# Sparse attention with items that hold both key-value heads

## The reference, cut to what matters

```python
s = jnp.einsum('bqhgd,bchd->bqhgc', q_nope, kc) * scale
_, l, e = masked_softmax(s, avail[None, :, None, None, :])
p_cmp = e / jnp.maximum(l, TINY)
o_cmp = jnp.einsum('bqhgc,bchd->bqhgd', p_cmp, vc)
...
nsa = gates[:, :, 0] * o_cmp + gates[:, :, 1] * o_slc + gates[:, :, 2] * o_win
```

## Time and profile before

| | us |
|---|---|
| median of 3 runs | 2389.52 |
| lowest, highest | 2380.57, 2398.0 |
| the profiled execution, its own time | 2398.31 |
| its span | 2396.5 |

### The profile page before, as it was taken

How to read it: one execution, slowest core, us unless ns; L and a number is a source line. 1 busy time by engine, 2 the same in 40 slices (tenths; PEclk the granted TensorE clock), 3 DMA queues, 4 the chain that set the end, 5 groups by cost and what they waited for, 6 DMA issues and landing times.

```text
span 2396.5 us, 19995 instructions
## 1 busy us (share of the span) xinstructions
PE 1824.3 (76%) x6099; PEld 884.4 (37%) x6099; DVE 1466.1 (61%) x3339; ACT 560.5 (23%) x1754; POOL 721.5 (30%) x612
## 2 busy tenths in 40 slices
PE   7998798776887779678797786779765778656675
PEld 5575455642333222133342233334321445422221
DVE  1554520386877783677469745854974555556966
ACT  1001320112232231242222311422221222222222
POOL 0031000004454542234344522433432222223452
PEclk9975556898999999889899888889987777778988
DMA  6231003409999999999999998999999988889997
GB/s 213 90 99 46 1 0 106 141 1 375 421 418 421 422 400 421 380 370 403 412 421 409 400 420 323 383 366 399 406 375 373 342 326 300 342 347 376 391 391 301
DMA packets 152163, 750.89 MB, mean 313 GB/s; under 512 B 22092, under 2 KB 54744, under 8 KB 72056
## 3 DMA queue, kind: packets, MB, share of 16 engines
q0 software_dynamic: 84480, 608.21, 62.8%
q1 hardware_dynamic: 67576, 141.41, 16.3%
HBM read 743.96 MB, written 5.60 MB: 313 GB/s over the span
## 4 chain that ended last, share of the span: by engine, by line
DMA 26%; PE 22%; DVE 17%; issue 6%; ACT 2%; SPq 1%; PEldq 1%; POOL 1%; DVEq 1%; PEld 0%; ACTq 0%; POOLq 0%
DMA uv<-in_experts_dram,slots 18%; PE ps L2261 12%; DVE uv L2169 6%; PE ps L583 3%; PE ps L1106 2%; DMA sample_cache<-in_odd_w_in_dram 2%; PE ps L1078 2%; DMA last_w<-in_odd_w_in_dram 1%; DMA sample_w<-in_peer_w_q_dram 1%; DVE acc L2183 1%; SPq L1876 1%; PEldq L2297 1%; ACT diag L2237 1%; POOL uv L2151 1%; DMA last_rows<-in_peer_sub_keys_dram 1%
## 5 line engine op out<-in xcount | busy, mean ns | idle before, releaser
L2261 PE MATMUL ps<-uv,diag 128*128 128x512 f32 (+1 forms) x1880 | 982.5, 664 | 275.7 <-ACT diag L2237 211.5
L2151 POOL DMA_INDIRECT uv<-in_experts_dram,slots x576 | 689.3, 1197 | 1487.6 <-PE ps L2261 1021.0
L2169 DVE CUSTOM_DVE_ANT_0 uv<-uv,x 128x1024 f32<-128x1024 f32 x512 | 622.5, 1225 | 295.8 <-DMA uv<-in_experts_dram,slots 236.7
L2261 PEld LDWEIGHTS ps<-uv,diag 128*128 128x128 f32 (+1 forms) x1880 | 352.8, 200 | 821.1 <-issue 473.0
L2215 ACT ACTIVATE gelu<-dot 128x2 f32<-128x2 f32 x288 | 58.6, 203 | 1098.3 <-DVE dot L2169 1098.1
L2237 ACT ACTIVATE diag<-const,wgt 128x128 f32<-128x128 f32 (+1 forms) x470 | 165.0, 387 | 9.4
L2224 ACT ACTIVATE wgt<-gate,gelu 128x1 f32<-128x1 f32 x576 | 138.0, 287 | 38.9 <-SPq L2367 14.7
L2183 DVE SCALAR_TENSOR_TENSOR acc<-uv,wgt,acc 128x1024 f32<-128x1024 f32 x101 | 129.5, 1282 | 1.0 <-ACT wgt L2224 1.0
L2169 DVE CUSTOM_DVE_ANT_0 uv<-uv,xs 128x1024 f32<-128x1024 f32 x64 | 78.1, 1225 | 76.7 <-DMA uv<-in_experts_dram,slots 75.2
L583 PE MATMUL ps<-last_w,xT 128*128 128x512 f32 x160 | 77.2, 627 | 9.2 <-DMA last_w<-in_odd_w_in_dram 7.5
L583 PE MATMUL ps<-first_w,xT 128*128 128x512 f32 x160 | 75.6, 611 | 3.1 <-DMA first_w<-in_odd_w_in_dram 3.1
(11 more groups left out here) (425 smaller groups left out, 1910.0 us busy)
## 6 DMA issues: line engine op xcount, KB each, us to landing
sample_cache<-in_cache_dil_kv_dram SPq DMA_DIRECT2D x64, 256.0 KB, 10.4
cache<-in_even_w_in_dram SPq DMA_DIRECT2D x12, 1024.0 KB, 6.8
first_w<-in_odd_w_in_dram SPq DMA_DIRECT2D x12, 1024.0 KB, 11.1
last_w<-in_odd_w_in_dram SPq DMA_DIRECT2D x12, 1024.0 KB, 12.2
sample_cache<-in_odd_w_in_dram SPq DMA_DIRECT2D x12, 1024.0 KB, 17.2
uv<-in_experts_dram,slots POOLq DMA_INDIRECT x576, 11.1
uv<-in_peer_w_q_dram SPq DMA_DIRECT2D x8, 1024.0 KB, 12.0
first_w<-in_peer_w_q_dram SPq DMA_DIRECT2D x8, 1024.0 KB, 10.2
```

The source lines that it names most:

```text
L2151: self.k.nc.gpsimd.indirect_dma_start(out=self.uv[:, s % RING, :], out_offset=None, in_=self.table, in_offset=bass.IndirectOffsetOnAxis(ap ...
L2169: ins = nc.vector.tensor_tensor_reduce(self.uv[:, s % RING, 0:D], self.uv[:, s % RING, 0:D], x, 1.0, 0.0, ALU.mult, ALU.add, self.dot[:, g ...
L2261: last = nc.tensor.matmul(k.bank(c)[0:m, :], self.diag[:, s % RING, 0:m], self.uv[:, s % RING, D + 512 * c:D + 512 * (c + 1)], start=(j == ...
```

## The change

A new stage, `paired_attention`, takes the place of `attention` for the sparse attention alone; `attention` stays as it is for the dilated attention. An item now holds both heads, with their groups side by side. In the first tile an item has 8 groups of 128 keys; in the second 4 groups of 256 (two query heads of each key-value head), so that a branch has two items there; the compressed branch has 8 groups in both. The sample's items have 2 groups. That makes 11 items: 3, 5 and 3. Scores of head 0 go to the first bank of the pair, those of head 1 to the second. Score products and value products are listed with the two heads in turn. The scores of item i+2 are divided: one half before the transposes of item i, the other behind them. An item's turned probabilities come in sets, one or two rounds each, and a set's value products follow the transposes of the next set. `nsa_probT` has four places instead of two.

```diff
+def paired_attention(k, name, items, bufs, before_scores=()):
...
+    def scores(i, half=None):
+        if i < n_items:
+            count = len(items[i]["scores"])
+            mid = count // 4 * 2
+            a, b = {None: (0, count), 0: (0, mid), 1: (mid, count)}[half]
+            for at in range(a, b, 4):
+                ticks.append([("scores", i, at, min(at + 4, b))])
...
+    def turn(s):
+        for r in sets[s][2]:
+            ticks.append([("turn", r), ("copy", r)])
...
+    for i in range(n_items):
+        ticks.append([("normalise", i)])
+        scores(i + 2, 0)
+        turn(sets_of[i][0])
+        scores(i + 2, 1)
+        mask_and_exp(i + 2)
+        for s in sets_of[i]:
+            if s != sets_of[i][-1]:
+                turn(s + 1)
+            count = len(sets[s][3])
+            for at in range(0, count, 8):
+                ticks.append([("values", s, at, min(at + 8, count))])
+        ticks.append([("leave", i)])
...
+            for c0, cn, lhsT, rhs, start, stop in items[i]["scores"][a:b]:
+                last = nc.tensor.matmul(score_banks(i)[:, c0:c0 + cn], lhsT, rhs, start=start, stop=stop)
...
+            if r >= slots:
+                act.wait_ge(summed, set_of_round[r - slots] + 1)
...
-                for kv in range(KV):
-                    p = slice(64 * kv, 64 * kv + 64)
...
-                        scores=[(0, 128, g * nk, nk, q[p, g, cols(t)], keys, True, True) for g in range(GR)],
...
+                apart = max(nk, 128)
+                per = 512 // apart
+                for first in range(0, GR, per):
+                    scores = [(512 * kv + apart * g, nk, q[p, first + g, cols(t)], keys(p), True, True)
+                              for g in range(per) for kv, p in enumerate(halves)]
...
+                        sets = [(0, min(nk, 128), [range(0, GR), range(GR, 2 * GR)],
+                                 [(out[p, to], value(0, p), kv, lambda pT: pT, begin, end) for kv, p in enumerate(halves)])]
...
+            scores = [(512 * kv, width, qb[p, b].rearrange("p g t -> p (g t)"), keys(p, b), b == 0, b == DEC_B - 1)
+                      for b in range(DEC_B) for kv, p in enumerate(halves)]
...
+                sets += [(128 * j, 128, [range(KV)], [(dst(p, b), cache[n][:, b, j, 128 + p.start:128 + p.stop], 0, own(kv, b), False, False)
+                                                      for b in range(DEC_B) for kv, p in enumerate(halves)]) for j in range(NPG)]
...
+        bufs = (k.sbuf("nsa_prob", [128, 3, 1024], ctx=outer), k.sbuf("nsa_probT", [128, 4, 512], ctx=outer),
+                k.sbuf("nsa_small", [128, 4, 3, KV * GR], ctx=outer))
+        alone(k, spread, paired_attention(k, "nsa", items, bufs, [(queries_spread, 1)]))
```

More of the change, by code:

```diff
@@ L1737, in attend @@
         items = []
+        halves = [slice(64 * kv, 64 * kv + 64) for kv in range(KV)]
+        prompt_gates = lambda t, br, heads: gates[:, t, :].rearrange("p (a k g) -> p a k g", a=3, k=KV)[:, br, :, heads]
+        branches = ((1, "slc", SLC0), (2, "win", WIN0), (0, "cmp", CMP0))
         for t in range(2):
-            bank = 6 + t
-            out = k.bank(bank).rearrange("p (g q) -> p g q", q=128)
-            for br, n in ((1, "slc"), (2, "win"), (0, "cmp")):
-                for kv in range(KV):
-                    p = slice(64 * kv, 64 * kv + 64)
[L1744 to L1758, removed]
-                        scores=[(0, 128, g * nk, nk, q[p, g, cols(t)], keys, True, True) for g in range(GR)],
-                        count=None, gate=gate, parts=parts, leave=leave))
@@ L1761, in attend @@
-        out = k.bank(6)[:, 0:GR * NS]
[L1762 to L1782, removed]
@@ L1783, in attend @@
-        alone(k, spread, attention(k, "nsa", items, attention_buffers(k, "nsa", 1024, 512, outer), before_scores=[(queries_spread, 1)]))
+            out = k.bank(6 + t)
+            for br, n, base in branches:
+                q = qT["nope" if n == "cmp" else "rope"]
+                keys = lambda p: kc[p, 0, :] if n == "cmp" else kT[n][p, NS:NS + 128 * (t + 1)]
+                value = lambda j, p: vc[:, 0, p] if n == "cmp" else h[:, j, base + 128 + p.start:base + 128 + p.stop]
+                nk = NBLK if n == "cmp" else 128 * (t + 1)
+                apart = max(nk, 128)
[3 more added lines that the diff above has]
+                              for g in range(per) for kv, p in enumerate(halves)]
+                    to = slice(128 * first, 128 * (first + per))
+                    begin, end = n == "slc", n == "cmp"
+                    if per == GR:
+                        sets = [(0, min(nk, 128), [range(0, GR), range(GR, 2 * GR)],
+                                 [(out[p, to], value(0, p), kv, lambda pT: pT, begin, end) for kv, p in enumerate(halves)])]
+                    else:
+                        sets = [(128 * j, 128, [range(0, 2 * per)],
+                                 [(out[p, to], value(j, p), 0, lambda pT, a=128 * per * kv, b=128 * per * (kv + 1): pT[:, a:b],
+                                   begin and j == 0 and first == 0, False) for kv, p in enumerate(halves)])
+                                for j in range(t + 1)]
+                    leave = [(catT[:, 4:8, cols(t)], out.rearrange("p (g q) -> p g q", q=128))] if n == "cmp" else []
+                    items.append(dict(groups=KV * per, n=nk, apart=apart, scores=scores, sets=sets, leave=leave,
+                                      mask=k.c("cmp_mask")[:, t, :] if n == "cmp" else k.c("causal")[:, t, 0:nk],
+                                      gate=prompt_gates(t, br, slice(first, first + per))))
@@ new lines, in attend @@
+        out = k.bank(6)[:, 0:GR * NS]
+        own = lambda kv, b: (lambda pT: pT[:, 128 * kv:128 * (kv + 1)].rearrange("p (g t) -> p g t", t=NS)[:, :, DEC_T * b:DEC_T * (b + 1)])
+        dst = lambda p, b: out[p, :].rearrange("p (g t) -> p g t", t=NS)[:, :, DEC_T * b:DEC_T * (b + 1)]
+        for br, n, base in branches:
+            qb = q_b["nope" if n == "cmp" else "rope"]
+            keys = (lambda p, b: kc[p, 1 + b, :]) if n == "cmp" else (lambda p, b: kTs[n][p, b, :])
+            nk, width = (NBLK, NBLK) if n == "cmp" else (PAST + NS, PAST)
+            scores = [(512 * kv, width, qb[p, b].rearrange("p g t -> p (g t)"), keys(p, b), b == 0, b == DEC_B - 1)
+                      for b in range(DEC_B) for kv, p in enumerate(halves)]
+            if n == "cmp":
+                sets = [(0, NBLK, [range(KV)], [(dst(p, b), vc[:, 1 + b, p], 0, own(kv, b), False, True)
+                                                for b in range(DEC_B) for kv, p in enumerate(halves)])]
+            else:
+                scores += [(512 * kv + PAST, NS, q_new[p].rearrange("p g t -> p (g t)"), kT[n][p, SMP], True, True)
+                           for kv, p in enumerate(halves)]
+                value = lambda p: slice(base + 128 + p.start, base + 128 + p.stop)
+                sets = [(PAST, NS, [range(KV)], [(out[p, :], h[0:NS, 2, value(p)], 0, lambda pT, kv=kv: pT[:, 128 * kv:128 * (kv + 1)],
+                                                  n == "slc", False) for kv, p in enumerate(halves)])]
+                sets += [(128 * j, 128, [range(KV)], [(dst(p, b), cache[n][:, b, j, 128 + p.start:128 + p.stop], 0, own(kv, b), False, False)
+                                                      for b in range(DEC_B) for kv, p in enumerate(halves)]) for j in range(NPG)]
+            leave = [(catT[:, 4:8, SMP], out.rearrange("p (g t) -> p g t", t=NS))] if n == "cmp" else []
+            items.append(dict(groups=KV, n=nk, apart=512, scores=scores, sets=sets, leave=leave,
+                              mask=None if n == "cmp" else k.c("new_causal"),
+                              gate=gates_s[:, KV * br:KV * (br + 1)].rearrange("p (k o) -> p k o", o=1)))
```

133 lines of the change are left out of this document (added).

## The result

| | before | after |
|---|---|---|
| median of 4 runs each, side by side | 2388.3 | 2350.4 (2342.2 to 2354.0) |
| the profiled execution's own time | 2398.3 | 2354.0 |
| its span | 2396.5 | 2352.2 |
| first score to the end of the stage's last copy | 142.8 | 92.9 |
| from there to the end of the span | 2001.7 | 2007.5 |

The changed kernel is faster by 1.7%, ratio 0.983 [0.980, 0.986]. The forecast was 2346 within 2322 to 2370.

A forecast was written before the change was run, and what follows sets the result against it. Sparse-attention stage bounds: TensorE waits in the first tile, mask-exponentials-copy ring in the second, TensorE in the sample. Pieces sum to 104.0 us, less 5 for clock: 99 against 142.8, gain 44, median 2346, range 2322 to 2370.

The forecast's parts named there:

- Where the time lies: Sparse-attention stage: a stretch of its own, 142.8 us of work; everything behind it moves by what it wins or loses.
- A pair costs one product: All score and value products: two on different array halves cost one; the bound without overlap is twice that.
- halves take turns: Rival, whole stage: products cost as today, no pairing; stage 147.5 less some clock, median 2392; chance 0.06.
- each alternation drains: Rival, all 208 products: each change of half exposes 0.2, 42 us more; stage 189, median 2436; chance 0.03.
- Column halves load one after another: Rival, sample's 168 small value products: keep 0.11 each, 9 us more; stage 108, median 2355; chance 0.12.
- The order: Whole stage, 11 items worked through in the new order with their waits: 104.0 us at half clock.
- First transposes at 10.0: First tile: scores 2.1, mask 2.7, exponentials 3.2, normalise 1.85 and gaps put the first transposes 10.0 us after the first score.
- a turn of the ring: Second tile: mask, exponentials, copy queued behind them, values, scores and transposes before the next mask; 9.9 us against 11.0.
- The 0.35: Everywhere on the path: a result is seen 0.35 us after its last product starts.
- The clock: Sample's two long score runs: granted clock rises, then falls at waits; 5 us off 20 of products, stage 104 to 99.
- The rival of a full clock: Rival, whole stage: full clock throughout halves the products on the path; stage 77, gain 66, median 2324; chance 0.18.
- The four places of `nsa_probT`: Buffers for turned probabilities, four instead of two: remove a wait that did not bind, worth nothing.

The follow-up runs named there:

- the second timing: The changed kernel, unaltered, timed again in more rounds beside the kernel before: median 2341.7 of 5 runs against 2393.0, ratio 0.979; stage 91.5 us.
- the best version: Changed kernel with undivided scores and all transposes and copies of item i before mask and exponentials of item i+2: median 2317.5 against 2390.7, ratio 0.969; stage 69.7.
- the kernel with one half: Changed kernel with both heads' scores and values on partitions 0 to 63, same order and items: median 2385.0 against 2391.0, ratio 0.997; stage 132.0.

## Why the prediction was right, and where its steps were off

*Where the time lies*: right, as far as the runs can tell, which is to about 5 us. The stage is a stretch of its own and what follows moves with it: 51.3 of 51.2 us arrive in the second timing (142.8 − 91.5), 73.2 of 73.0 in the best version, 46 of 49.9 over all nine runs of the change. A profiled pair doesn't show that: the same code behind the stage differed by 11 us between two profiles.

*A pair costs one product*: right for all kinds, by the rows above and by the kernel with one half. What the prediction did not see is that this holds only while the halves alternate within about four matmuls. It read the 3.10 at 252.07 against 3.4, which leaves the tail out; the kernel on one half has 3.78. The rivals "halves take turns" (2392) and "each alternation drains" (2436) are refuted by the same rows. "Column halves load one after another" (2355) fell with 64 matmuls in 3.60 against 7.01 on one half, 0.056 each; what fell is its price, 0.11 for every load. The Trainium skill, "TensorE: Matmul & The Clock Gate", Part 3, lets a weight load overlap only where its row group differs; here all rows are shared and the measurement decides against that rule. The Trainium skill, "TensorEngine Tiling (Array Packing)", Key Properties, has only a change of mode drain, not one of tile; the 3.79 agrees.

*The order*: right, to a few tenths where the clock stood at half. First transposes at 10.0 (forecast 10.0); a turn of the ring 9.84 (9.9); the second tile 26.3 (27.0). The 0.35 that the forecast counts from the start of a last product belongs behind that product's own 0.21 to 0.44, as in the earlier trace rows: 304.82 + 8 × 0.436 is 308.31, and the mask starts at 308.63. Its sums take it so.

*The clock*: this term failed. I took 5 us off 104; the stage came out 11.1 under it. By part the difference from half clock is 2.4 in the first tile (28.9 against 31.3), 0.7 in the second, 6.8 in the sample (20.9 against 27.7) and 1.2 in the rest (16.85 against 18.0). The last is not clock, as the windows view shows 0.50 there; it is the rest priced too dear. That leaves 9.9 for the clock, nearly twice what I took, if all else was priced right; the rows of the sample bear it out in the main (the second sixteen of an item in 2.00 instead of 3.79, twice). I put it into the sample's scores alone, and the first tile has its share, with 0.74. The rival of a full clock (77) had the direction, not the size: the second tile stayed at 0.56 and the end at 0.50.

*The total*: 2346 lies 4 under one median and 4 over the other. With the stage's real gain on the basis of the forecast it would have been 2340. That the first median came so near is in part luck: the clock's missing 6 us of gain met a first set of runs in which 12 of the stage's 49.9 did not arrive.

*What I took as given*: the prediction worked out the divided scores and the ring correctly, and never asked what they cost against the nearest other order. That was 23 us, some clock included, nearly half of the gain again. The copy's part could have been read from the earlier trace rows: the copy waits for exponentials of an item it has nothing to do with. The four places of `nsa_probT`, priced at nothing, were not tried against two.

## What to carry to other kernels

Where products use only half of the array's rows or columns, list the two halves in turn, product by product: a pair then costs one, but of products grouped by half only some four matmuls overlap at each change. When TensorE's products become cheap, look at once for the ring that is left, and put the small copy that TensorE waits for ahead of long work for a later item. Judge a change in one stage by the stage's own length, and let medians of several runs say whether the rest follows.

## What the runs showed of the hardware

The overlap between halves reaches about four matmuls at a change of half: 3.4, 3.7 and 3.7 were hidden, for three kinds of products whose pace differs fourfold (0.45, 0.22 and 0.11 us).

The granted clock did not follow how full TensorE was. Two stretches of the kernel after, in the windows view:

```profile
310.60:317.43 6.83, 4.50 (x38) 3.09 (x36) 2.35 (x7) 2.20 (x6) 0.00 (x0) 1.00 0.01 2
...
327.67:344.69 17.02, 16.03 (x198) 12.80 (x198) 2.65 (x13) 3.13 (x11) 0.00 (x0) 0.50 0.01 2
```

It rose to 2.4 GHz behind sixteen paired scores without a pause and stayed there through a stretch with TensorE busy for 4.50 of 6.83 us. It stayed at 1.2 GHz in the last stretch, which is mostly value products of 16 columns, with TensorE busy for 16.03 of 17.02.

Nor does the use of both halves decide it. With the scores alone on one half it read 0.50 in the whole stage, through four sixteens of 7.19 us without a pause. With scores and values on one half it read 0.50 as well over the first such scores, and then rose:

```profile
320.30:327.00 6.70, 6.70 (x16) 5.09 (x16) 0.00 (x0) 0.00 (x0) 0.00 (x0) 0.50 0.00 0
...
341.00:350.00 9.00, 9.00 (x47) 7.07 (x45) 0.00 (x0) 1.05 (x2) 0.00 (x0) 1.00 0.00 0
```

What decides it was not tried.
